# Scaled logits with a running minimum in one VectorE instruction, and seven-step gate spacing, in a hybrid encoder step

## The reference

```
h = RMSNorm(x);  proj = h @ w_in
mixer A:  s = (q_nope.k_nope + q_rope.k_rope) * A_SCALE         # A_SCALE = 96 ** -0.5, 8 heads
          o_A = softmax(where(mask, s, -inf)) @ v_A
mixer B:  an indexer chooses 128 keys for each query (72 for the sample)
          s = (q.k) * B_SCALE over the chosen keys              # B_SCALE = 64 ** -0.5, 8 heads
          o_B = softmax(s) @ v_B
x = x + (sigmoid(g_A) * (o_A @ w_o_a) + sigmoid(g_B) * (o_B @ w_o_b)) @ w_out
x = x + PEER(RMSNorm(x))        # 8 heads x 16 of 16384 experts for each token, rows u and v of 1024 each
```

## Time and profile before

| what | value |
|---|---|
| median of 3 runs | 1849.74 us (1841.86 to 1852.79) |
| the profiled execution's own time | 1844.66 us |
| its span, first to last instruction | 1842.9 us |
| mean granted TensorE clock | 0.764 of full speed |
| busy: PE, DVE, ACT, POOL | 1250.1, 1317.2, 567.5, 524.2 us |
| HBM traffic | 697.5 MB, mean 378 GB/s over the span |
| queue of the expert rows | 570.5 MB, 74.4% of the 16 DMA engines' span |

### The profile page before, as it was taken

One profiled execution on the slowest core, in us unless ns is written; L12 is line 12 of the kernel. 1 busy time (PEld: TensorE's weight loads), 2 busy tenths in 40 slices (PEclk: granted clock), 3 DMA queues, 4 the chain that ended last, 5 costly groups with the idle time before them and its releaser, 6 DMA issues.

```text
span 1842.9 us, 26343 instructions
## 1 busy us (share of the span) xinstructions
PE 1250.1 (68%) x8990; PEld 688.1 (37%) x8990; DVE 1317.2 (71%) x3906; ACT 567.5 (31%) x1997; POOL 524.2 (28%) x569
## 2 busy tenths in 40 slices
PE   8989747678787565778877485878877444434343
PEld 3666623345444222445445132555535111111111
DVE  5661495889767477899767667998757768686754
ACT  3331223424322233333412333333423222222222
POOL 0100032333322322322322322422323333333332
PEclk9999859778888778788898587888998555555555
DMA  6325499999999999999999999998999999999997
GB/s 261 100 81 174 158 426 406 384 425 424 426 424 419 420 416 386 389 425 407 408 423 421 424 393 408 423 402 319 419 422 423 426 427 426 426 426 423 426 423 299
DMA packets 119668, 697.51 MB, mean 378 GB/s; under 512 B 18015, under 2 KB 21150, under 8 KB 49390
## 3 DMA queue, kind: packets, MB, share of 16 engines
q0 software_dynamic: 78848, 570.53, 74.4%
q1 hardware_dynamic: 36974, 122.88, 17.5%
q10 hardware_dynamic: 3712, 2.43, 0.4%
HBM read 692.70 MB, written 3.02 MB: 378 GB/s over the span
## 4 chain that ended last, share of the span: by engine, by line
DMA 36%; PE 25%; DVE 24%; issue 5%; ACT 3%; POOL 1%; ACTq 0%; DVEq 0%; POOLq 0%
DMA rows<-in_peer_uv,index 27%; DVE rows L2342 10%; PE ps_v L1600 5%; PE ps_f L1422 3%; DMA wch<-in_w_out 3%; PE ps_f L1472 3%; DMA wch<-in_w_row 3%; PE ps_f L1216 3%; PE ps_f L1451 2%; PE ps_h L1580 2%; DMA wch<-in_peer_wq 2%; PE ps_f L1437 2%; DMA wch<-in_w_uq 2%; DVE score L2066 1%; DVE best L2065 1%
## 5 line engine op out<-in xcount | busy, mean ns | idle before, releaser
L1193 POOL DMA_INDIRECT rows<-in_peer_uv,index x544 | 514.3, 945 | 1221.7 <-PE ps_v L1600 1021.6
L2342 DVE CUSTOM_DVE_ANT_0 rows<-rows,ps_h 128x1024 f32<-128x1024 f32 x544 | 657.7, 1220 | 281.2 <-DMA rows<-in_peer_uv,index 237.7
L1600 PE MATMUL ps_v<-rows,diag 128*32 128x256 f32 x4352 | 431.3, 512 | 474.0 <-ACT diag L1902 473.6
L1600 PEld LDWEIGHTS ps_v<-rows,diag 128*32 128x32 f32 x4352 | 125.1, 132 | 728.9 <-ACT diag L1902 624.9
L1893 ACT ACTIVATE tan<-arg 128x2 f32<-128x2 f32 x272 | 55.4, 204 | 830.0 <-DVE arg L2352 804.7
L1896 ACT ACTIVATE weight<-tan,lead 128x1 f32<-128x1 f32 x544 | 180.8, 379 | 9.2
L1902 ACT ACTIVATE diag<-sel,weight 128x32 f32<-128x32 f32 x544 | 140.7, 305 | 0.0
L1422 PEld LDWEIGHTS ps_f<-bufh,wch 128*128 128x128 f32 x768 | 115.8, 236 | 22.0 <-issue 19.6
L1422 PE MATMUL ps_f<-bufh,wch 128*128 128x128 f32 x768 | 122.8, 326 | 0.0
L1216 PE MATMUL ps_f<-wch,bufh 128*128 128x512 f32 (+1 forms) x192 | 82.1, 571 | 16.6 <-DMA wch<-in_w_row 16.6
L1451 PE MATMUL ps_f<-wch,bufb 128*128 128x512 f32 x96 | 50.2, 657 | 18.2 <-DMA wch<-in_w_out 18.2
(11 more groups left out here) (359 smaller groups left out, 1665.5 us busy)
## 6 DMA issues: line engine op xcount, KB each, us to landing
wch<-in_w_gate SPq DMA_DIRECT2D x60, 512.0 KB, 8.1
wch<-in_w_row SPq DMA_DIRECT2D x36, 512.0 KB, 10.6
wch<-in_w_o SPq DMA_DIRECT2D x32, 512.0 KB, 7.8
wch<-in_w_out SPq DMA_DIRECT2D x32, 512.0 KB, 11.1
wch<-in_peer_wq SPq DMA_DIRECT2D x32, 512.0 KB, 10.0
rows<-in_peer_uv,index POOLq DMA_INDIRECT x544, 13.8
w_tok<-in_w_tok SPq DMA_DIRECT2D x4, 1640.0 KB, 13.4
wch<-in_w_uq SPq DMA_DIRECT2D x6, 384.0 KB, 7.0
```

The costliest lines, as they stand in the source:

```text
L1193: pool.indirect_dma_start(rows[c % RING][:, :, :].rearrange("p a d -> p (a d)"), None, io.peer_uv[:, :], at).then_inc(s_uv[c % RING], 16)
L1600: ins = nc.tensor.matmul(ps_v[GROUP * a:GROUP * (a + 1), :], diag[:, c % DRING, :], rows[c % RING][:, 1, QD * a:QD * (a + 1)], start=False ...
L2342: v.tensor_tensor_reduce(out=u, in0=u, in1=ps_h[:, :], scale=1.0, scalar=0.0, op0=ALU.mult, op1=ALU.add, accum_out=dots[:, c % KEEP:c % KE ...
```

## The change

In the logits step of the loop over tiles, the reduction multiplies by minus the softmax scale as it adds the bias, and keeps the minimum in place of the maximum. That minimum is minus the scaled maximum, which the exponential takes as its bias; it reads the stored logits with scale -1. The separate multiplication, the semaphore s_max and VectorE's wait on its own reduction are gone. The 32-query steps of the sample (few_logits, line 2126) keep the two instructions. In later fronts gate pairs are placed seven ticks apart: pair j at 7j + 2 and 7j + 4, its tanh at 7j + 5.

```diff
     def gate_at(p, k):
-        n = 6 if p else 9
+        n = 7 if p else 9
         j, r = divmod(k, n)
         return (gates_of(p)[j], 0 if r == n // 3 else 1) if 0 <= j < len(gates_of(p)) and r in (n // 3, 2 * n // 3) else None
     def tanh_at(p, k):
-        n = 6 if p else 9
+        n = 7 if p else 9
...
-        s_max = sem("s_max")
...
-                act.wait_ge(s_max, a + 1)
+                act.wait_ge(s_logit, a + 1)
...
                 nc.scalar.activation(prob[a % 2][0:q, 0:nk], logit[a % 2][0:q, 0:nk], ACT.Exp,
-                                     bias=mx[0:q, a % 2, 1:2], scale=A_SCALE if x == 0 else B_SCALE,
-                                     accum_out=total[0:q, x, h:h + 1]).then_inc(s_prob, 1)
+                                     bias=mx[0:q, a % 2, 1:2], scale=-1.0, accum_out=total[0:q, x, h:h + 1]).then_inc(s_prob, 1)
...
-                step(v.tensor_tensor_reduce(out=shaped(i, logit[a % 2]), in0=scored(i, u), in1=bias, scale=1.0, scalar=NEG,
-                                            op0=ALU.add, op1=ALU.max, accum_out=mx[0:q, a % 2, 0:1]), s_logit)
-                v.tensor_scalar(mx[0:q, a % 2, 1:2], mx[0:q, a % 2, 0:1],
-                                -(A_SCALE if kind == "mla" else B_SCALE), None, ALU.mult).then_inc(s_max, 1)
+                v.tensor_tensor_reduce(out=shaped(i, logit[a % 2]), in0=scored(i, u), in1=bias,
+                                       scale=-(A_SCALE if kind == "mla" else B_SCALE), scalar=-NEG,
+                                       op0=ALU.add, op1=ALU.min, accum_out=mx[0:q, a % 2, 1:2]).then_inc(s_logit, 1)
```

## The result

The changed kernel took 1851.98 us (median of 13 runs, 1847.62 to 1859.75), beside it the kernel before 1844.64 us (13 runs, 1838.83 to 1852.79). The ratio is 1.0038, 95% interval [1.0022, 1.0053]: slower by 0.38%, small against my bound of 0.5% but clearly not the gain of 0.57% that I forecast. The figure of 1852.0 us lies on the upper end of my range only because the three runs of before that I started from lay high; by the ratio the same three would have gone to 1849.74 x 1.0038 = 1856.8. The profiled execution took 1851.06 us against 1844.66.

A forecast was written before the change was run, and what follows sets the result against it. Beyond the first front, time was to be won only where DMA engines run dry, with VectorE and TensorE waiting in turn. 1.1 + 2.7 + 1.0 + 2.5 + 3.2 = 10.5 us off 1849.7 gave 1839.2 us, range 1829 to 1852.

The forecast's parts named there:

- my bound of 0.5%: The smallest difference from no change that the measurement was taken to tell, about 0.5% or 9.2 us.
- What bounds the kernel: Beyond the first front, time can only be won where DMA engines run dry: 3.7 us third front, 14.4 fourth.
- Part 1, the step: VectorE's logits step loses the multiplication and its wait on its own reduction: 0.19 us a step, 0.07 as lower value.
- 33 steps on the chain, 6.3 us: Logits steps said to count: 6 in the first front, 14 in the third, 13 in the fourth.
- The first front's 1.1 us: Gain from six logits steps on the first front's chain, between 96 and 151 us.
- Part 2, the step that failed: Gate pairs seven ticks apart: in mixer A's ticks TensorE has room, so the move was costed at nothing.
- the second front, which I had called covered: At 425 GB/s, nothing to win: full DMA engines hide its 16 logits steps, worth 3.0 us if uncovered.
- The 3.2 us for one gate fewer: In mixer B's ticks 32 to 40, four gates become three: 3.2 us, bounds 0 and 6.5.
- 2.5 + 3.2: Fourth front's forecast gain: 2.5 us from 13 logits steps and 3.2 us from one gate fewer.
- The clock rival: Thinner gates idle TensorE, its clock falls and gives back the gain: 1846 to 1850 us, no gain; chance 0.28.
- The odd ticks: Gates at odd ticks stand right ahead of the next scores, delaying VectorE's logits: 1858.5 or 1866.7 us; chance 0.11.
- Loads and last pair: Later w_gate and w_o loads, and last gates at ticks 51 and 53 near the last transposes, costed at nothing.

The follow-up runs named there:

- e12: The changed kernel with four idle gate-sized pieces added in each later front, at ticks 14, 20, 28 and 34: 1.0006 of the kernel before.
- e15: e14 with four idle gate-sized pieces added in each later front, at ticks 12, 18, 24 and 30: 0.9966 of the kernel before.
- e3: The changed kernel with every odd-tick gate pair one tick later, so all pieces stand at even ticks: 1.0040 of the kernel before.
- e7: The changed kernel with gate pairs starting at ticks 2, 8, 14, 20, 26, 32, 42 and 48: 0.9986 of the kernel before.
- e1: The changed kernel with gate pairs six ticks apart as before, so only the logits step is new: 0.9983 of the kernel before.
- e14: e1 with the last gate pair alone moved from ticks 44 and 46 to 50 and 52: 0.9970 of the kernel before.
- e13: e1 with the gate pieces at ticks 20, 22, 26 and 28 cut from eight matmuls to one: 1.0036 of the kernel before.
- e9: e1 with each w_gate chunk of later fronts loaded two chunks later, gates unmoved: 0.9969 of the kernel before.

## Why the prediction was wrong

- *What bounds the kernel.* Right: beyond the first front, time goes where the DMA engines run dry, and start and shortage together give the profiled times of all kernels within 1.2 us (e12: 0.8 - 11.0 = -10.2, measured -10.3; e15: 2.1 - 6.3 = -4.2, measured -4.5; worst e3 and e7).
- *Part 1, the step.* The price was right (0.19 us, no slower reduction). The count was not: 33 steps on the chain, 6.3 us, were to come; e1 as a whole gives 1844.6 x 0.0017 = 3.1 us, with an interval of 7.2 us gained to 1.1 lost. That VectorE instructions lie on the chain didn't make their savings whole gains: in e1's trace VectorE waits 6.2 us for scores in the fourth front, as before, and 8.5 in the third, where before had 3.3. The first front's 1.1 us can't be seen: its end scatters by 6 us from profile to profile.
- *Part 2, the step that failed: "In mixer A's ticks, where VectorE leads, TensorE has room and I cost the move at nothing."* TensorE does have room, and giving it more has a price: from e1, where the gates stand at six, to the changed kernel, where they stand at seven, the time grows by 0.55%. Among the kernels without idle pieces, all five with eight pieces in ticks 5 to 34 have 1.0038 or more, all eight with ten or twelve whole ones 1.0009 or less. With two pieces fewer TensorE is at 1.2 GHz oftener (mean clock 0.764 in e1, 0.755 after); the attention's own matmuls take 14.0 us more than in e1 (16.6 more than before); VectorE waits 29.8 us for scores instead of 18.2 (9.8 before); and the second front, which I had called covered, loses 4.2 us of full DMA time. The third loses 5.1 against before, but 3.3 of these are there in e1 too.
- *The 3.2 us for one gate fewer, and the fourth front.* The four gates among mixer B's first ticks did become three, and the shortage of the fourth front went from 14.7 to 13.8 us, where 2.5 + 3.2 were to come. It is 12.9 to 18.6 us in eleven of the fifteen experiments' profiles, and lowest in e14 (6.8); what makes that dip these runs don't settle.
- *The rivals.* The clock rival (0.28) had the mechanism, and in direction it was right. It was mis-sized: "two more gates in each of the third and fourth front", 6.9 us, and about as much for the scores near them, which was only to eat the gain. It is not the gates that got colder (they became 9.0 us cheaper) but the attention around them. The Trainium skill, TensorE: Matmul & The Clock Gate, Part 1, has idling throttle the clock and activity release it; e12 and e13 agree, from both sides (mean clock 0.755 to 0.772 with idle pieces added, 0.764 to 0.747 with work taken out). The odd ticks (0.11) had the right sign for a wrong reason.
- *Loads and last pair.* Costed at nothing, rightly: e9 and e14.

## What to carry to other kernels

In a pipeline where TensorE is the helper, its idle time is not free room: taking matmuls out of a stretch can make the others in it slower. Before moving work off TensorE, read the granted clock of the stretch that it leaves, and price the small matmuls that stay at 1.2 GHz, not only the moved ones. And where two engines wait for each other in turn, a saving on one is worth what the other allows; test the parts alone, for here one part hid most of what the other cost.

## What the runs showed of the hardware that I had not expected

- Four idle pieces in each of three fronts, 192 matmul records more in all, made a kernel 0.32% faster (e12 against the changed one), and 168 records fewer made one 0.53% slower with TensorE busier, 1257.5 us against 1251.5 (e13 against e1).
- Over all 314 executions of the sixteen kernels and the one before, taken each against the mean of its own kernel, time and mean granted clock go together (correlation -0.47): an execution with a clock lower by 0.01 takes about 6 us longer. This alone doesn't say which of the two leads. e12 and e13 change the work, and clock and time both follow; the steps from the clock to the time they leave in part open, as said above.
